# A hybrid transformer block on one core: the queries' two parts as one 512-column matmul, and the keys' second part formed by GpSimd

## The reference

```python
def project(t):
    q, k, v = jnp.split(t @ w_qkv, 3, axis=-1)          # 16 heads of 128
    return rms_norm(q, q_g), rms_norm(k, k_g), v         # norm over each head's 128
q, k, v = project(h)        # h:  256 latent tokens after adaLN
qc, kc, vc = project(hc)    # hc: 256 context tokens; their queries are not used
s_lat = q @ k.T * scale + bias ; s_lat = where(ok, s_lat, -inf)
s_ctx = q @ kc.T * scale
p = softmax(concat([s_lat, s_ctx]))
y = (p_lat @ v + p_ctx @ vc) @ w_o
```

## Time and profile before

| | |
|---|---|
| time, median of 3 runs | 2528.85 us (2528.56 to 2531.67) |
| time of the profiled execution | 2528.97 us |
| its span, first to last instruction | 2527.0 us |
| mean granted TensorE clock | 1.000 |
| TensorE busy, share of the span | 2502.4 us (99%) |
| VectorE busy | 1625.4 us (64%) |
| ScalarE busy | 1264.2 us (50%) |
| GpSimd busy | 155.8 us (6%) |

### The profile page before, as it was taken

One profiled execution on the slowest core, in us unless ns is written; L12 is line 12 of the kernel. 1 busy time (PEld: TensorE's weight loads), 2 busy tenths in 40 slices (PEclk: granted clock), 3 DMA queues, 4 the chain that ended last, 5 costly groups with the idle time before them and its releaser, 6 DMA issues.

```text
span 2527.0 us, 34842 instructions
## 1 busy us (share of the span) xinstructions
PE 2502.4 (99%) x13734; PEld 2133.3 (84%) x13734; DVE 1625.4 (64%) x2384; ACT 1264.2 (50%) x1945; POOL 155.8 (6%) x160
## 2 busy tenths in 40 slices
PE   7999999999999999999999999999999999999999
PEld 4688899998898888888888898988888888888887
DVE  2576887886689986566665576666555554545554
ACT  3244433334575554355554455555666665443443
POOL 1001100010021110001110000001000000000000
PEclk9999999999999999999999999999999999999999
DMA  9953777775669995666665666555655556666665
GB/s 334 355 184 116 230 247 240 245 249 178 208 195 272 286 270 191 196 189 188 190 189 185 191 167 181 170 173 173 172 169 151 163 160 190 183 186 189 188 187 167
DMA packets 459202, 511.45 MB, mean 202 GB/s; under 512 B 36867, under 2 KB 327778, under 8 KB 458528
## 3 DMA queue, kind: packets, MB, share of 16 engines
q1 hardware_dynamic: 456032, 501.11, 64.9%
q0 software_dynamic: 2864, 8.11, 1.1%
q10 hardware_dynamic: 144, 0.02, 0.0%
HBM read 506.93 MB, written 2.22 MB: 201 GB/s over the span
## 4 chain that ended last, share of the span: by engine, by line
PE 93%; DVE 2%; ACT 2%; SPq 1%; issue 1%; DMA 1%; DVEq 0%; ACTq 0%
PE PG L1023 17%; PE PG L1025 17%; PE PG L1024 17%; PE PG L1013 11%; PE PG L1016 6%; PE PG L1032 4%; PE PG L1033 4%; PE PG L1034 4%; PE PS L1144 1%; PE PS L892 1%; ACT wh L1286 1%; SPq L803 1%; PE PS L1211 1%; PE PG L907 1%; DVE wl L1705 1%
## 5 line engine op out<-in xcount | busy, mean ns | idle before, releaser
L1705 DVE TENSOR_TENSOR wl<-raw,wh 128x1024 fp32r<-128x1024 f32 (+1 forms) x745 | 911.4, 1228 | 682.7 <-ACT wh L1286 681.0
L1286 ACT ACTIVATE wh<-raw 128x1024 fp32r<-128x1024 f32 (+1 forms) x745 | 785.5, 1056 | 843.9 <-PE PG L1025 563.6
L1013 PE MATMUL PG<-FHL,wh 128*128 128x512 f32 x1248 | 392.1, 395 | 0.3 <-DVE wl L1705 0.3
L1023 PE MATMUL PG<-wh,HHL 128*128 128x512 f32 x832 | 331.0, 398 | 0.4 <-DVE wl L1705 0.4
L1025 PE MATMUL PG<-wl,HHL 128*128 128x512 f32 x832 | 324.8, 390 | 0.0
L1024 PE MATMUL PG<-wh,HHL 128*128 128x512 f32 x832 | 324.1, 390 | 0.0
L1016 PEld LDWEIGHTS PG<-FHL,wl 128*128 128x128 f32 x1248 | 234.4, 188 | 55.4
L1016 PE MATMUL PG<-FHL,wl 128*128 128x256 f32 x1248 | 245.1, 278 | 0.0
L1013 PEld LDWEIGHTS PG<-FHL,wh 128*128 128x128 f32 x1248 | 190.2, 189 | 0.7 <-DVE wl L1705 0.5
L1025 PEld LDWEIGHTS PG<-wl,HHL 128*128 128x128 f32 x832 | 156.1, 188 | 33.5
L1023 PEld LDWEIGHTS PG<-wh,HHL 128*128 128x128 f32 x832 | 156.3, 188 | 31.1 <-DVE wl L1705 0.8
(11 more groups left out here) (434 smaller groups left out, 4419.6 us busy)
## 6 DMA issues: line engine op xcount, KB each, us to landing
raw<-in_w_in SPq DMA_DIRECT2D x208, 512.0 KB, 3.7
raw<-in_w_up SPq DMA_DIRECT2D x344, 256.0 KB, 3.4
raw<-in_w_ada SPq DMA_DIRECT2D x128, 512.0 KB, 5.2
raw<-in_w_down SPq DMA_DIRECT2D x84, 512.0 KB, 4.4
raw<-in_w_qkv SPq DMA_DIRECT2D x80, 512.0 KB, 4.7
first<-in_w_ada SPq DMA_DIRECT2D x78, 256.0 KB, 7.2
raw<-in_w_o SPq DMA_DIRECT2D x32, 512.0 KB, 3.9
raw<-in_w_in SPq DMA_DIRECT2D x64, 256.0 KB, 3.1
```

The source lines that it names most:

```text
L1013: pe.matmul(to, hi[:, 128 * j:128 * j + 128], flat(FHL[:, step.k, :, :]), start=step.first, stop=False, skip_group_check=True)
L1023: pe.matmul(dst, xh[:, cols], hi, start=step.first and j % per == 0, stop=False, skip_group_check=True)
L1286: ac.activation(wh[n % NSPL][:, 0:src.shape[1]], src, ACT.Copy).then_inc(S["hi"], 1)
L1705: dv.tensor_tensor(wl[n % NSPL][:, 0:x], src, wh[n % NSPL][:, 0:x], ALU.subtract).then_inc(S["lo"], 1)
```

## The change

The queries' three matmuls of 256 columns per block become two: the weights' high part moves both parts of x in one matmul of 512 columns (`XHL[:, 0:2, step.k, 0:T]`, two pieces of 256), the weights' low part moves the high part of x alone. The result then has two halves per block. A new job `q_sum`, on step 0 of the next product, adds them: ScalarE copies the second half to `QF` (the memory of `QL`), VectorE adds the first half and frees `PG`. The square, `QH` and `QL` are then made from `QF`. `q_out`'s three phases move: phase 0 from step 0 to 2, phase 1 from 3 to 4, phase 2 from 4 to 6. `k_mul` phase 3 is dropped from VectorE; GpSimd forms `KL` for both heads of a group after the mask of the group's second head.

```diff
         nxt, late = (("k", g, 0) if g > 1 else ("q", g + 1, 0)), 7 if g == 2 else 0
-        P.put(nxt, late, "q_out", g, 0)
-        P.put(nxt, 3 + late, "q_out", g, 1, 1)
-        P.put(nxt, 4 + late, "q_out", g, 2)
+        P.put(nxt, late, "q_sum", g, 0)
+        P.put(nxt, 2 + late, "q_out", g, 0)
+        P.put(nxt, 4 + late, "q_out", g, 1, 1)
+        P.put(nxt, 6 + late, "q_out", g, 2)
...
-            for phase, n in enumerate((0, 1, 2, 2)):
+            for phase, n in enumerate((0, 1, 2)):
                 P.put(to, at_mul[j] + n, "k_mul", (g, j), phase, phase == 0)
...
+    QF = [at(f"QF{i}", [128, 2, T], F32, 49 + 2 * i) for i in range(2)]
...
+    Q_ROWS = [[512, 128], [256, 2], [64, 4]]
+
+    def q_half(g, n):
+        return result("q", g)[:, :, T * n:T * n + T].rearrange("p j (a n) -> p j a n", n=64)
...
+            g = h // 2
+            if s:
+                for j in range(2):
+                    w.wait_ge(S["k_hi"], 2 * g + j + 1)
+                    po.tensor_tensor(KL[g % 2][:, j, :], KBf[g % 2][:, j, :], KH[:, j, :],
+                                     ALU.subtract).then_inc(S["k_lo"], 1)
...
+            if name == "q":
+
+                for j in range(2):
+                    pe.matmul(ps[:, j, :], hi[:, 128 * j:128 * j + 128], XHL[:, 0:2, step.k, 0:T], start=step.first, stop=False,
+                              skip_group_check=True)
+                for j in range(2):
+                    end = pe.matmul(ps[:, j, 0:T], lo[:, 128 * j:128 * j + 128], xh, start=False, stop=step.last,
+                                    skip_group_check=True)
+            elif name == "up":
...
-                    w.wait_ge(*out_done("q", g))
+                    w.wait_ge(S["q_lo"], g + 1)
...
+            elif job == "q_sum":
+                g, b = key, key % 2
+                w.wait_ge(*product_done("q", g))
+                if g >= 2:
+                    w.wait_ge(*full(use("attn", 2 * g - 3, 0, 1)))
+                ac.activation(rev(QF[b], 0, Q_ROWS), q_half(g, 1), ACT.Copy).then_inc(S["q_low"], 1)
...
-                w.wait_ge(*product_done("q", g))
-                ps = q_result(g).rearrange("p (a n) -> p a n", n=64)
-                ac.activation(rev(q_squares(g), 0, [[512, 128], [64, 8]]), ps, ACT.Square).then_inc(S["q_sq"], 1)
+                w.wait_ge(*out_done("q", g))
+                ac.activation(q_squares(g)[:, :], flat(QF[b][:, :, :]), ACT.Square).then_inc(S["q_sq"], 1)
...
-                ac.activation(rev(QH[b], 0, [[512, 128], [64, 8]]), ps, ACT.Copy, scale=gqk[:, 0:1]).then_inc(S["q_hi"], 1)
+                ac.activation(QH[b][:, :, :], QF[b][:, :, :], ACT.Copy, scale=gqk[:, 0:1]).then_inc(S["q_hi"], 1)
...
+            elif job == "q_sum":
+                g, b = key, key % 2
+                w.wait_ge(S["q_low"], g + 1)
+                end = dv.tensor_tensor(rev(QF[b], 0, Q_ROWS), q_half(g, 0), rev(QF[b], 0, Q_ROWS), ALU.add)
+                end.then_inc(out_sem("q", g), 1)
...
-                rows = [[512, 128], [64, 8]]
-                dv.scalar_tensor_tensor(out=rev(QL[b], 0, rows), in0=q_result(g).rearrange("p (a n) -> p a n", n=64),
-                                        scalar=gqk[:, 0:1], in1=rev(QH[b], 0, rows), op0=ALU.mult,
-                                        op1=ALU.subtract).then_inc(out_sem("q", g), 1)
+                dv.scalar_tensor_tensor(out=QL[b][:, :, :], in0=QF[b][:, :, :], scalar=gqk[:, 0:1], in1=QH[b][:, :, :],
+                                        op0=ALU.mult, op1=ALU.subtract).then_inc(S["q_lo"], 1)
...
-            elif (job, phase) == ("k_mul", 3):
-                (g, j), u = key, use("k_mul", key, 0)
-                w.wait_ge(*emptied(u))
-                w.wait_ge(S["k_hi"], 2 * g + j + 1)
-                dv.tensor_tensor(KL[g % 2][:, j, :], KBf[g % 2][:, j, :], KH[:, j, :], ALU.subtract).then_inc(S["k_lo"], 1)
```

More of the change, by code:

```diff
@@ L473 @@
         "ada_pe", "ada_dv", "ada_row", "side", "side0", "side1", "side2", "side3", "out0", "out1",
-        "dve", "act", "pool", "xtload", "gbias", "res", "xsq", "xr", "xf_hi", "xh_hi", "up0", "sh_hi", "sh_lo", "fin_p", "fin_d", "fin_hi", "fin_lo", "sel", "k_r", "k_rh", "k_rl", "q_hi", "k_hi", "k_lo", "mod_t", "mod_hi", "mod_lo", "gain", "scales", "maxed", "exped", "weighed",
+        "dve", "act", "pool", "xtload", "gbias", "res", "xsq", "xr", "xf_hi", "xh_hi", "up0", "sh_hi", "sh_lo", "fin_p", "fin_d", "fin_hi", "fin_lo", "sel", "k_r", "k_rh", "k_rl", "q_low", "q_hi", "q_lo", "k_hi", "k_lo", "mod_t", "mod_hi", "mod_lo", "gain", "scales", "maxed", "exped", "weighed",
         "o_hi", "biased", "masked", "l_mask", "q_sq", "k_sq", "rq",
@@ L696, in result @@
         return PG[turn(name, g) % 2]
-    def q_result(g):
-        return result("q", g)[:, 0, :]
+    Q_ROWS = [[512, 128], [256, 2], [64, 4]]
+    def q_half(g, n):
+        return result("q", g)[:, :, T * n:T * n + T].rearrange("p j (a n) -> p j a n", n=64)
     def product_done(name, g):
@@ L1008, in product @@
             hi, lo = weights(step)
-            if name == "up":
+            if name == "q":
[6 more added lines that the diff above has]
+            elif name == "up":
                 dst = [ps[:, j, :] for j in range(hi.shape[1] // 128)]
@@ L1867, in piece @@
                 w.wait_ge(S["q_hi"], g + 1)
-                if g >= 2:
-                    w.wait_ge(*full(use("attn", 2 * g - 3, 0, 1)))
-                rows = [[512, 128], [64, 8]]
-                dv.scalar_tensor_tensor(out=rev(QL[b], 0, rows), in0=q_result(g).rearrange("p (a n) -> p a n", n=64),
-                                        scalar=gqk[:, 0:1], in1=rev(QH[b], 0, rows), op0=ALU.mult,
-                                        op1=ALU.subtract).then_inc(out_sem("q", g), 1)
+                dv.scalar_tensor_tensor(out=QL[b][:, :, :], in0=QF[b][:, :, :], scalar=gqk[:, 0:1], in1=QH[b][:, :, :],
+                                        op0=ALU.mult, op1=ALU.subtract).then_inc(S["q_lo"], 1)
             elif (job, phase) == ("q_out", 2):
```

## The result

The changed kernel takes 2535.23 us (median of 14 runs, 2534.28 to 2538.25), the kernel before 2529.56 (2528.28 to 2532.22): a ratio of 1.0023, 95% interval 1.0015 to 1.0030. It is slower by 5.7 us, which is clear of no change by this interval and just over the 0.2% that the prediction had counted as no change. The time lies inside the forecast range of 2526.5 to 2535.5, but only 0.3 us under its upper end, and 4 us above the single number. The profiled execution took 2534.46 for a span of 2532.5, against 2528.97 and 2527.0: 5.5 more.

A forecast was written before the change was run, and what follows sets the result against it. TensorE's own work was taken to bound the kernel; 2.95 us saved less 5.2 of new waits gave +2.2 on the profiled 2528.97, so 2531 us, range 2526.5 to 2535.5.

The forecast's parts named there:

- rival (b): Keys' subtractions on GpSimd take 1.9 us and hold VectorE's weight split up: +6.6, 2535.6 us; chance 0.15.
- Bound and matmuls: TensorE's work sets the time; a query step falls from 0.720 to 0.697 us, 0.37 a group.
- the 2.95: Queries' product on TensorE: 0.023 us saved a step over 128 steps, 2.95 us in all.
- The queries' way out: Copy, add, square before TensorE's sums: VectorE's add runs late, TensorE waits 1 to 1.5 us in groups 3, 4, 5.
- the sum for group 4: TensorE's sums of the squares in group 4: squares ready at 358.56 against 357.18 due, 1.4 us late.
- the 2.2 of the sum: All groups together: 2.95 us saved less 5.2 of new waits, +2.2 us on the profiled execution.
- the 0.2% bound: About 0.2% (5.1 us) is told from no change; slower, over 2533.9 us, had chance 0.20.
- GpSimd and VectorE: Keys' subtraction moved to GpSimd frees VectorE, but contention costs its split 0.76; 0.2 us of 1.44 kept.
- Rival (a): VectorE is relieved, GpSimd contention hardly bites, the whole 1.44 us shift arrives: -1.6, 2527 us; chance 0.25.
- the full 1.44: Without the keys' subtractions VectorE could split the next weights at 405.05, 1.44 us earlier, absent GpSimd contention.
- Groups 0 to 2: Groups 0 and 2 leave room and keep 0.37 us each; group 1's 0.3 lateness eats its 0.37.
- Rival (c): Queries' 512-column matmuls save nothing, step stays 0.72 us: 2532.6, up to 2534 us; chance 0.07.

The follow-up runs named there:

- e2: Changed kernel with TensorE's waits for the square in groups 3, 4 and 5 filled by 5, 7 and 4 matmuls of ones: 2531.16 us, ratio 1.0008.
- e4: e1 with the queries' product as six matmuls of 256 columns a step again: 2527.77 us, ratio 0.9996 to the kernel before.
- e1: Changed kernel with the sums of the queries' squares behind step 6 instead of 4, inverse root behind 8 instead of 6: 2525.71 us, ratio 0.9986.
- e3: Changed kernel with the keys' second part back on VectorE in its old place: 2536.25 us, ratio 1.0027 to the kernel before.
- e5: Changed kernel with the sums of the queries' squares back behind step 3 instead of step 4: 2559.85 us, ratio 1.0120.

## Why the prediction was right, and where it was short

The time lies in the range, and the mechanism at the sums of the squares was right; that the range held is in part luck. Its upper end, 2535.5, was set for rival (b), GpSimd holding VectorE up, which did not happen; what filled it was a fall of the clock that stands nowhere in the prediction.

The single number was 2531.2, the profiled execution 2534.46. By group, in us against the kernel before, worked out from the start of the scores behind each group's sums (TensorE's timelines of the kernels):

```
group   forecast   changed   with the waits filled (e2)
0 to 2    -0.7       -0.1       -0.1
3         +1.2       +1.1       +1.1
4         +1.4       +4.1       +0.6
5         +1.0       +0.6       +0.6
6         -0.4       -0.4       -0.4
7         -0.3       +0.1        0
```

- **Bound and matmuls.** TensorE's work sets the time, and a query step went from 0.720 to 0.696. Right, though the 2.95 came through as 2.1 (e4 against e1), in full only from group 3 on.
- **The queries' way out.** Right in mechanism and place: the waits stand in the three groups named, behind an add that stands behind the adaLN tiles. e1 shows it by taking only this away. In size group 3 came out within 0.1 of the sum, group 5 had been taken 0.4 too dear, and group 4, as it is with the clock kept up (e2), 0.8 too dear.
- **The step that was short: the sum for group 4.** It counted the wait and not what TensorE does afterwards. The wait of 1.64 is followed by six microseconds at 1.2 GHz, 3.4 us (e2). No rival held it either. Without it (e2) the stage comes to 1.8 against the 2.2 of the sum, and that nearness is luck too: groups 4 and 5 cost 1.2 less than taken, groups 0 to 2 and 7 gave 0.9 less. The fall puts the result over the 0.2% bound, where 0.2 of the chance had been put.
- **GpSimd and VectorE.** The hold-up beside GpSimd was as large as taken: the split grew by 0.8, against 0.76 beside the mask. Measured against TensorE's own place (the start of the scores in the queries before), the add came 0.2, 0.6 and 0.5 us earlier in groups 3, 4 and 5 than L1871 had, where 0.2 was taken; that is part of why groups 4 and 5 cost less. The subtraction took 1.29, not 1.5 to 1.9, so rival (b) falls; the scores never waited. Rival (a) falls too, since the full 1.44 did not arrive.
- **Groups 0 to 2.** Groups 0 and 2 were taken at their full saving, 0.7 together; the three gave 0.1, since TensorE waits there for VectorE's split (the line below, from the kernel after) and 0.25 at group 1's sums. In e1, where the wait for the split stays and the one at the sums is gone, they give 0.8.

```profile
172.75 0.73 PE L1022 MATMUL PG<-XHL,wh 128*128 128x512 f32 x2 [0.44 <-DVE wl L1728]
```

- **Rival (c)** falls: a step took 0.696.

What stays open is which waits bring the clock down: 1.04 did in e3 and did not in the changed kernel's profile, nor did 1.28 there, while 0.95 did in e5. The kernel before has a wait as long, 1.07 at a transpose (262.46 us), and no fall; the kernel after has it too, at a clock of 1.00:

```profile
262.31 1.36 PE L1153 MATMUL PS<-ident,SB 128*128 128x128 f32 x8 [1.07 <-DVE SB L1967]
```

## What to carry to other kernels

A chain across three engines (copy, add, square) has to be placed by the queue of its slowest link, here VectorE behind a block of other work, and TensorE's piece at its end hung far enough behind it; the cost was two numbers in a schedule. On a kernel where TensorE never stops, price a wait with what follows it: 1.64 us of idling cost 3.4 more at the lower clock, though not every such wait did. A gap that can't be closed can be filled with matmuls of no use, which cost nothing there and kept the clock.

## What the runs showed of the hardware that was not expected

The granted clock fell to 0.50 right behind one wait of 1.64 us in a stage that had run at 1.00, stayed there some six microseconds of dense matmuls, and did not fall with the same gap filled (e2). In e3 it fell behind 1.04 as well, in e5 behind 0.95. The GpSimd pass over 128x512 took 1.29 us in all 16 places, and the VectorE split that met it in groups 4 and 5 took 2.06 instead of 1.23; a VectorE pass of 0.16 took 1.16 and ended with GpSimd's. A moving operand of two pieces of 256 columns ran as fast (0.696 us a step) as one of 512 in a row (0.697).
